# Attention levels of a hybrid diffusion step: exponent differences on the Pool engine, in three rotating buffers

## The reference, cut to what matters

```
bcum = cumsum(log f)                       # per channel, within a chunk
att[t, s] = sum_d q[t, d] * k[s, d] * exp(bcum[t, d] - bcum[s, d])     for s <= t
o = att @ v + (q * exp(bcum)) @ S          # S: state at the chunk's start
S = S * exp(btot) + (k * exp(btot - bcum))^T @ v
```

## Time and profile before

| what | value |
|---|---|
| time, median of 3 runs | 1663.26 us (1659.13 to 1664.9) |
| the profiled execution's own time | 1655.0 us |
| its span, first to last instruction | 1653.4 us |
| PE, DVE, ACT, POOL busy | 88%, 31%, 18%, 7% of the span |
| mean granted TensorE clock | 0.943 of full speed |
| the 14 levels | from 407.5 to 549.0 us |

### The profile page before, as it was taken

One profiled execution on the slowest core, in us unless ns is written; L12 is line 12 of the kernel. 1 busy time (PEld: TensorE's weight loads), 2 busy tenths in 40 slices (PEclk: granted clock), 3 DMA queues, 4 the chain that ended last, 5 costly groups with the idle time before them and its releaser, 6 DMA issues.

```text
span 1653.4 us, 46602 instructions
## 1 busy us (share of the span) xinstructions
PE 1451.6 (88%) x20350; PEld 1100.7 (67%) x20351; DVE 520.7 (31%) x1101; ACT 295.8 (18%) x511; POOL 122.5 (7%) x195
## 2 busy tenths in 40 slices
PE   5998899766888999999992899989989898989894
PEld 3677689746767766666451667867767676767672
DVE  4814880357777432111335001101101010101014
ACT  2214001232222430000120111111111111111112
POOL 0060120100000000000002000000000000000002
PEclk9999899677999999999995899999999999999997
DMA  8276241520311002131119891791885989899885
GB/s 356 83 237 259 60 82 52 211 107 27 116 64 52 13 26 89 39 149 73 58 37 371 317 369 25 286 361 25 311 335 175 394 315 395 308 368 347 315 315 197
DMA packets 87176, 319.20 MB, mean 193 GB/s; under 512 B 11057, under 2 KB 11313, under 8 KB 86865
## 3 DMA queue, kind: packets, MB, share of 16 engines
q1 hardware_dynamic: 72288, 270.05, 43.0%
q0 software_dynamic: 14832, 48.34, 9.5%
HBM read 283.46 MB, written 32.80 MB: 191 GB/s over the span
## 4 chain that ended last, share of the span: by engine, by line
PE 69%; DMA 13%; DVE 10%; issue 3%; SPq 3%; ACT 2%; POOL 1%; POOLq 0%; DVEq 0%; ACTq 0%
PE ps L1839 19%; DMA expert_w<-in_w_up 11%; PE ps L1454 10%; PE ps L1824 9%; PE ps L1442 6%; PE ps L1742 4%; PE ps L1778 4%; PE ps L1687 3%; PE ps L1590 2%; DMA weight_ring<-in_stream 2%; PE ps L1625 2%; PE ps L1644 1%; SPq L481 1%; PE ps L1807 1%; SPq L487 1%
## 5 line engine op out<-in xcount | busy, mean ns | idle before, releaser
L1839 PEld LDWEIGHTS ps<-x_block_t,expert_w 128*64 128x64 f32 x14336 | 457.1, 140 | 168.1 <-issue 103.1
L1839 PE MATMUL ps<-x_block_t,expert_w 128*64 128x64 f32 x14336 | 462.1, 224 | 44.3 <-DMA expert_w<-in_w_up 41.7
L1387 DVE TENSOR_TENSOR act_t<-silu_tmp,ps 128x64 f32<-128x64 f32 x224 | 49.5, 221 | 579.7 <-ACT silu_tmp L826 579.7
L1824 PE MATMUL ps<-expert_w,act_t 128*64 128x512 f32 x896 | 229.2, 601 | 0.0
L1454 PE MATMUL ps<-h_t,weight_ring 128*128 128x320 f32 x640 | 176.7, 432 | 0.0
L1454 PEld LDWEIGHTS ps<-h_t,weight_ring 128*128 128x128 f32 x640 | 120.7, 190 | 52.6 <-issue 5.7
L826 ACT ACTIVATE silu_tmp<-ps 128x64 f32<-128x64 f32 x224 | 50.0, 223 | 578.9 <-PE ps L1839 578.9
L1442 PE MATMUL ps<-h_t,weight_ring 128*128 128x320 f32 x512 | 141.3, 439 | 3.6 <-ACT h_t L641 3.6
L1442 PEld LDWEIGHTS ps<-h_t,weight_ring 128*128 128x128 f32 x512 | 98.7, 193 | 45.3 <-issue 5.6
L1687 PE MATMUL ps<-node_x 128*128 128x128 f32 x560 | 73.7, 290 | 29.0 <-DVE att L1155 14.8
L1687 PEld LDWEIGHTS ps<-node_x 128*128 128x128 f32 x560 | 69.1, 201 | 33.9 <-DVE att L1155 17.1
(11 more groups left out here) (323 smaller groups left out, 1340.1 us busy)
## 6 DMA issues: line engine op xcount, KB each, us to landing
expert_w<-in_w_gate SPq DMA_DIRECT2D x128, 512.0 KB, 14.3
expert_w<-in_w_up SPq DMA_DIRECT2D x128, 512.0 KB, 15.4
expert_w<-in_w_down SPq DMA_DIRECT2D x128, 512.0 KB, 15.0
weight_ring<-in_stream SPq DMA_DIRECT2D x98, 512.0 KB, 5.1
x_sorted<-zero POOLq DMA_DIRECT2D x18, 512.0 KB, 18.4
x_block<-x_sorted POOLq DMA_DIRECT2D x29, 256.0 KB, 6.6
y_sorted<-y_block POOLq DMA_DIRECT2D x56, 128.0 KB, 5.1
y_sorted<-zero POOLq DMA_DIRECT2D x9, 512.0 KB, 28.5
```

Source lines behind the costliest of these rows:

```text
L1387: vec.tensor_tensor(act_t[:, f, :], silu[:, f % 2, :], ps[:, 2 + f % 2, 0:MB], ALU.mult)\
L1824: last = mm(ps[MB * half:MB * half + MB, 4, :], act_t[:, f, :], w_slot[3 * f + 2][:, 4 * half:4 * half + 4, :].rearrange("p k c -> p (k c) ...
L1839: last = mm(ps[cols, 2 * w + f % 2, 0:MB], w_slot[3 * f + w][:, k, cols], x_blk_t[:, k, :], start=(k == 0), stop=(k == KD - 1))
```

## The change

The differences move from VectorE to GpSimd: `subtract(s)` issues two instructions on Pool for each level, straight into the tile that the level's products will overwrite. Instead of one `exp_tmp` and two `node_x` there are three tiles in rotation, `node_x1`, `exp_tmp`, `node_x0` (`node_buf(s)`), in which the difference, its exponential and the products follow each other in place. Pool may write a tile when TensorE has finished the level that used it three levels earlier (`for_dve` at `node_job(s - 3, CH - 1) + 1`). In VectorE's order only masked copies of level s-1, then `take_vectors(s - 1)`, then the products of level s are left. The sum `kf + kb` for the diagonal moves ahead of the states, into `exp_tmp`, and `take_diag` ahead of everything of the levels. On Pool, the output of `hg_new` stands behind the first two `subtract`, the load of `router_w` behind all 14.

```
+        def node_buf(s):
+            return (node_x[0], node_x[1], ex)[(s + 1) % 3]
...
+            def subtract(s):
+                d, l = STEPS[s]
...
+                if s == 1:
+                    pool.wait_ge(for_dve, V["diag"] + CH)
+                elif s >= 3:
+                    pool.wait_ge(for_dve, node_job(s - 3, CH - 1) + 1)
+                a0, a1 = (mid, left) if d == 0 else (left, mid)
+                nc.gpsimd.tensor_tensor(x[:, :, 0, :], a0, a1, ALU.subtract)
+                a0, a1 = (right, mid) if d == 0 else (mid, right)
+                nc.gpsimd.tensor_tensor(x[:, :, 1, :], a0, a1, ALU.subtract).then_inc(node_sub, 1)
+
+            pool.wait_ge(b_ready, 2)
+            pool.wait_ge(for_act, A["kt"] + 10)
+            subtract(0)
+            subtract(1)
             pool.wait_ge(states_ready, 1)
             for d in range(2):
                 pool.dma_start(hg_new[d, :, :, :].rearrange("h d v -> d h v"), st[:, d, SCH, :, :])\
                     .then_inc(hg_out, 16)
+            for s in range(2, len(STEPS)):
+                subtract(s)
             pool.dma_start(rw[:, :, :], router_w).then_inc(rw_in, 16)
...
             for n in range(len(STEPS)):
-                exp_in_place(3 + n)
+                act.wait_ge(node_sub, n + 1)
+                nc.scalar.activation(node_buf(n)[:, :, :], node_buf(n)[:, :, :], ACT.Exp).then_inc(e_exp, 1)
...
-                act.wait_ge(e_sub, 17 + d)
-                nc.scalar.activation(ex[:, :, :], (ff if d == 0 else fb)[:, :, :], ACT.Exp).then_inc(e_exp, 1)
+                act.wait_ge(for_dve, node_job(len(STEPS) - 3 + d, CH - 1) + 1)
+                nc.scalar.activation(node_x[d][:, :, :], (ff if d == 0 else fb)[:, :, :], ACT.Exp).then_inc(e_exp, 1)
...
+            vec.tensor_tensor(ex[:, :, :], kf[:, :, :], kb[:, :, :], ALU.add).then_inc(diag_ready, 1)
...
-            dve.wait_ge(for_act, A["kt"] + 10)
-            vec.tensor_tensor(node_x[1][:, :, :], kf[:, :, :], kb[:, :, :], ALU.add).then_inc(diag_ready, 1)
...
+            take_diag()
             for s, (d, l) in enumerate(STEPS):
...
-                if s == 0:
-                    take_diag()
-                else:
+                if s > 0:
                     take_nodes(s - 1)
+                    take_vectors(s - 1)
                 dve.wait_ge(e_exp, 3 + s)
...
                     .then_inc(node_ready, 1)
                 dve.wait_ge(node_ready, s + 1)
-                if s > 0:
-                    take_vectors(s - 1)
```

More of the change, by code:

```diff
@@ L314, in hybrid_step @@
         e_sub = sem("e_sub")
+        node_sub = sem("node_sub")
         e_exp = sem("e_exp")
@@ L405, in hybrid_step, with level_nodes @@
         STEPS = [(d, l) for d in range(2) for l in range(LEVELS)]
+        def node_buf(s):
+            return (node_x[0], node_x[1], ex)[(s + 1) % 3]
+        def level_nodes(t, l):
+            return t[:, :, :].rearrange("p h t -> p (h t)").rearrange("p (n w c) -> p n w c", w=2, c=(P // 2) >> l)
         RAW1 = (A["ada1a"], A["ada1a"] + 1, A["ada1a"] + 2, A["ada1b"])
@@ L561, in _ @@
                 .then_inc(hg0_in, 16)
+            def subtract(s):
+                d, l = STEPS[s]
+                half = (P // 2) >> l
+                b, x = level_nodes(ff if d == 0 else fb, l), level_nodes(node_buf(s), l)
+                left, right = b[:, :, 0, :], b[:, :, 1, :]
+                mid = (left[:, :, half - 1:half] if d == 0 else right[:, :, 0:1])\
+                    .broadcast_to((P, HEADS * TOK // (2 * half), half))
+                if s == 1:
[10 more added lines that the diff above has]
+            subtract(1)
             pool.wait_ge(states_ready, 1)
@@ L1161, in take_vectors @@
                     vectors(end_job(i), 16 + ADA_MID + GRP * i, end_tiles(i))
+            take_diag()
             for s, (d, l) in enumerate(STEPS):
[L1164 to L1179, removed]
-                if s == 0:
-                    take_diag()
-                else:
+                x, kv, qv = level_nodes(node_buf(s), l), level_nodes(kf if d == 0 else kb, l), level_nodes(q, l)
+                if s > 0:
                     take_nodes(s - 1)
+                    take_vectors(s - 1)
                 dve.wait_ge(e_exp, 3 + s)
-                note(vec.tensor_tensor(x[:, :, 0, :], (kv if d == 0 else qv)[:, :, 0, :], e[:, :, 0, :], ALU.mult))
-                vec.tensor_tensor(x[:, :, 1, :], (qv if d == 0 else kv)[:, :, 1, :], e[:, :, 1, :], ALU.mult)\
+                note(vec.tensor_tensor(x[:, :, 0, :], (kv if d == 0 else qv)[:, :, 0, :], x[:, :, 0, :], ALU.mult))
+                vec.tensor_tensor(x[:, :, 1, :], (qv if d == 0 else kv)[:, :, 1, :], x[:, :, 1, :], ALU.mult)\
                     .then_inc(node_ready, 1)
                 dve.wait_ge(node_ready, s + 1)
-                if s > 0:
-                    take_vectors(s - 1)
-            vec.nop().then_inc(e_sub, 1)
             take_nodes(len(STEPS) - 1)
@@ L1200, in _ @@
                 dve.wait_ge(e_exp, 17 + d)
-                vec.tensor_tensor(node_x[d][:, :, :], q[:, :, :], ex[:, :, :], ALU.mult).then_inc(qd_ready, 1)
+                vec.tensor_tensor(node_x[d][:, :, :], q[:, :, :], node_x[d][:, :, :], ALU.mult).then_inc(qd_ready, 1)
                 dve.wait_ge(qd_ready, d + 1)
-                if d == 0:
-                    vec.nop().then_inc(e_sub, 1)
             dve.wait_ge(g_ready, 1)
@@ L1675, in _ @@
                 for h in range(HEADS):
-                    last = mm(bank(job)[:, h * P:(h + 1) * P], node_x[1][:, h, c * P:(c + 1) * P],
+                    last = mm(bank(job)[:, h * P:(h + 1) * P], ex[:, h, c * P:(c + 1) * P],
                               q[:, h, c * P:(c + 1) * P], start=True, stop=True)
@@ L1680, in _ @@
                 pe.wait_ge(node_ready, s + 1)
-                x = node_x[s % 2]
+                x = node_buf(s)
                 for c in range(CH):
```

## The result

The changed kernel takes 1699.55 us (median of 4 runs, 1695.55 to 1701.56), the kernel before 1664.08 in the same session: ratio 1.0214, 95% interval 1.0178 to 1.025. A second session gave 1.0242 (1.0171 to 1.0314). It is slower, as forecast, by 35 to 40 us and not by 21. The profiled execution took 1695.55, its span is 1694.0, the granted clock 0.927 (before: 1655.0, 1653.4, 0.943).

What follows compares the result with a forecast made beforehand. Bound: a ring of TensorE matmuls and VectorE masked copies and products. Levels -3.5, head -5.0, tail -0.5, clock +8.4 gave -0.6; waits for Pool +13.5 and more clock +8.4 gave +21.3 on 1663.3: 1684.6 us, range 1655 to 1713.

Steps and rivals of the forecast that it cites:

- Sign and range: Whole kernel: slower with chance 0.78, time within 1655 to 1713 us.
- both halves: Rival, chance 0.30: in the levels, the pair of products waits for both Pool halves, delay 4.5 us; +46.8, 1710 us.
- The turns without contention: Levels without new engine contention: turns of 8.0, 13.1 and 9.1 us in a trio; levels together -3.5 us.
- the moved addition: Second of a trio: products stand behind the addition to `mod`, making the turn 13.1 us, 2 more than today.
- Head: Ahead of the levels: earlier `kf + kb` and a 5.1 us diagonal start level 0 at about 402.5, -5.0 us.
- the meeting: Products 0, 1, 3, 4, 6, 7, 9, 10 wait 2.1 us for Pool's first half; +13.5 us in total.
- Tail: Behind the levels: outputs start when `gate(0)` ends, -0.5 us.
- A half of `subtract`: One Pool instruction of 1280 elements takes 2.4 us, bounds 1.2 and 3.6.
- Who comes first: After a level's last matmul Pool starts in 0.04 us, ahead of the products, which come after 0.37 us.
- then, I take it, both products pass ahead of the second half: In the levels, VectorE waits only for Pool's first half, a delay of 2.1 us.
- The clock: Longer TensorE idle starts levels 2, 5, 8, 11 at half clock, +8.4 us, and levels 1, 4, 7, 10, +8.4.
- cover by the half projection: Thirds of a trio: the half projection outlasts the products, so only 1.0 us of each delay counts, 3 times.

Runs made afterwards that it cites:

- e2: Changed kernel, but Pool's subtraction for level s waits for the products of level s-2, not the matmuls of level s-3; 1662.72 us, ratio 0.9985.
- e5: As e2, but TensorE repeats 16 matmuls of 128x160 behind `select` in every second of a trio; 1654.61 us, ratio 0.9994.
- e3: Changed kernel with both edits: Pool waits for the products of level s-2, addition to `mod` back behind the products; 1641.86 us, ratio 0.9898.
- e6: As e3, with `kf + kb` in `node_x0`, so Pool need not wait for the diagonal before level 1's differences; 1630.88 us, ratio 0.9837.
- e4: Changed kernel, but Pool's subtraction waits for VectorE's last masked copy of level s-3, not TensorE's last matmul; 1683.73 us, ratio 1.0158.
- e1: Changed kernel with only the addition to `mod` put back behind the products; 1701.16 us, ratio 1.026.
- e8: Changed kernel, but Pool makes a level's differences in four instructions of 128x640 instead of two of 128x1280; 1684.64 us, ratio 1.0162.

## Why the prediction was right and wrong, step by step

**1. Sign and range: right.** 1699.55 lies in 1655 to 1713, between the forecast (1684.6) and "both halves" (1710). What happened between Pool and VectorE is what that rival says (chance 0.30), not what the forecast says (0.42). The range held because it was drawn to take the rival in.

**2. The turns without contention: right.** e2 and e5 show them. In e5's first profile level 0 alone of the levels 0 to 12 ran at half clock, as the prediction's -3.5 has it: its 13 turns of 130.8 are 3.3 below the 134.1 of before. Second of a trio 13.0 (predicted 13.1), first and third together 7.95 + 8.88 = 16.8 (17.1). The prediction set the moved addition against the turn of before, 11.2, and called it 2 us. Against the same kernel without the move (e3, 9.7) it costs 3.3; the other 1.5 are what freeing VectorE of the differences could have brought in this turn. Both readings are right, but the first hid that a kernel of 1642 was one wait and one line away.

**3. Head: right without the meeting.** Diagonal 5.08 (5.1), e6's level 0 is 5.1 us earlier than before, counted from the transposes (5.0). In the changed kernel products 0 meet `subtract(1)`, a pair of 6.5, and 1.5 are left (forecast: 5.0 - 2.1 = 2.9). The code load on Pool cost nothing that shows: Pool stood idle for 23.56 us ahead of its first subtraction and TensorE released it. Nor did the moved DMA issues. **Tail: right.** From level 13's last matmul to the outputs are 8.45 us, before 9.13: -0.7 (-0.5).

**4. A half of `subtract`: right.** 2.32 us (2.4 taken, bounds 1.2 and 3.6), and pieces of one element are no slower. But not every half is alike. Where the middle is the second operand, e6's undisturbed rows have 2.36, 2.40, 2.47, 2.59 and 2.90 for pieces of 64, 32, 16, 8 and 4, and 2.32 again for 2 and 1 (the other direction within 0.02); the other half takes 2.32 throughout. The Trainium skill (GPSIMD Engine Reference, Performance versus the Vector engine) led to an estimate of 2.8, which is 0.5 too long for most halves here. The 0.4 by which it exceeds the 2.4 taken would have raised the prediction's sum by 3.2 over eight meetings, not by "some 4".

**5. Who comes first: right.** Pool starts 0.29 us ahead of the products at the turn to level 1; the prediction had 0.33. The meetings are those named: levels 0, 1, 3, 4, 6, 7, 9, 10; those of 2, 5, 8, 11 miss. Masked copies are free.

**6. The step that failed: "then, I take it, both products pass ahead of the second half".** They do not. The engines change over between the two products, and in the 13 turns the pair waits for both halves: 6.8 to 7.5 us instead of 2.9, a delay of 4.0 at most meetings and not 2.1 (at level 0, where Pool was 0.75 us ahead, the pair took 6.5). The argument was even between the two engines (each has its next instruction queued), and the row that the prediction had, one Pool instruction against one of VectorE, could not tell it. The Trainium skill (SBUF — State Buffer, Who interferes with whom) has the exclusion for the whole of an instruction, and e4 and the changed kernel agree (3.61 and 3.87 us for a product of 1.48). In the 13 turns the longer pairs cost 16.3 us for levels 1, 4, 7, 10 (forecast 8.4) and, with some 0.8 of cover by the half projection, 10.2 for 3, 6, 9 (forecast 3.0).

**7. The clock.** Levels 2, 5, 8, 11 and 1, 4, 7, 10 started at half clock or soon fell to it, as forecast; from a level's start to its last masked copy they took 7.57, 6.43, 6.39, 6.10 and 6.44, 6.98, 7.71, 6.33, where 4.77 (5.24 at level 5) is the time at full clock. Together that is 6.9 and 8.4 too much, where 8.4 and 8.4 were forecast. The 2.1 a level was a little high, since the prediction set level 13's 7.45 against 4.7; level 12, with masked copies as long as level 13's, takes 5.2 at full clock. The longer idle from point 6 took the clock in levels 3, 6, 9 as well, 1.2 to 1.7 each against e3: +4.5, which the forecast had only under its rival.

The sum of the 13 turns: forecast -3.5 + 8.4 + 4 x 2.1 + 3 x 1.0 + 8.4 = +24.7. Points 6 and 7 add (16.3 - 8.4) + (10.2 - 3.0) + 4.5 - 1.5 = 18.1, which gives +42.8; measured +43.2. The "both halves" rival had +47.8. It was too high in three places: 1.7 for levels 1, 4, 7, 10 (a delay of 4.5 instead of 4.1), 1.8 for the clock of levels 3, 6, 9 (6.3 instead of 4.5) and 1.5 for that of 2, 5, 8, 11. Why the times differ by 35.5 in one session and about 40 in the next, with 43 in the profiled levels and 1.5 gained at the head, no run settles; I put it down to the spread ahead of the levels. Nothing shows a gain of the change's elsewhere.

## What to carry to other kernels

Work moved from VectorE to GpSimd is not parallel to VectorE's instructions with two SBUF operands, as these runs show for `TENSOR_TENSOR`. Give Pool a start event that puts it beside matmuls and copies out of PSUM (here the products' own semaphore, one wait, about -36 us). When two faults hide each other (e1 alone no gain in the time, e2 alone about -36, both about -55), undo them in both orders before you judge one. An order in which an engine waits for TensorE ahead of the work that TensorE waits for was paid twice here: 3.3 us of waiting and 2.3 of clock each time.

## What the runs showed of the hardware

- Pool and VectorE `TENSOR_TENSOR` instructions with two SBUF operands exclude each other and change over between instructions: pairs of 2.9 us took 6.8 to 7.5 with Pool first, 5.0 with VectorE first, 4.8 beside Pool instructions of half the size (e8); once the waiting engine was passed over three times (6.14 us).
- The row of the waiting instruction is long, not late: it counts as busy from its start. So Pool's rows of up to 3.84 us and VectorE's of up to 3.87 for one shape hold waits, and busy time doesn't tell of the loss. Pool's own length, undisturbed, runs from 2.32 to 2.90 us with the length of the pieces and the place of the repeated operand (point 4).
- VectorE instructions with one operand in PSUM (masked copies at 0.44, and the one product of the diagonal that met Pool, at 401.54 in the changed kernel, at 0.69) ran at their own length beside Pool.
- TensorE came back at full clock after 0.91 us of idle and at half after 3.19, with the same matmuls behind it. After 3.02 it began a level at 0.91 and stood at 0.50 from 1.5 us later on. After 2.31 it was at 1.00 in some profiles of a kernel and at 0.50 in another of the same kernel (e5, level 10), and after 3.50 it was at 1.00 once (e8, level 7).
